# First layer's modulation weights with outputs on partitions, and a first attention that starts on half of its normed features

## The reference, cut to what matters

```
c_act = silu(c)                                     # [1024]
mod = c_act @ ada_w[0] + ada_b[0]                   # 6*1024 outputs
sh_a, sc_a, gt_a, sh_m, sc_m, gt_m = split(mod, 6)
h = rms_norm(x, attn_norm[0]) * (1 + sc_a) + sh_a   # [512, 1024]
mix = diff_attention(h, ...)                        # 8 heads: project q, k, v, scores, softmax, values
x = x + gt_a * mix
h = rms_norm(x, mlp_norm[0]) * (1 + sc_m) + sh_m
x = x + gt_m * squared_relu_mlp(h)
```

## Time and profile before

| what | value |
|---|---|
| median of 3 runs | 2463.81 us (2459.13 to 2465.54) |
| the profiled execution: its own time | 2467.75 us |
| its span in the trace | 2465.9 us |
| PE busy | 2325.3 us (94%) |
| DVE busy | 1139.2 us (46%) |
| ACT busy | 503.7 us (20%) |
| mean granted TensorE clock | 0.968 |

### The profile page before, as it was taken

One profiled execution on the slowest core, in us unless ns is written; L12 is line 12 of the kernel. 1 busy time (PEld: TensorE's weight loads), 2 busy tenths in 40 slices (PEclk: granted clock), 3 DMA queues, 4 the chain that ended last, 5 costly groups with the idle time before them and its releaser, 6 DMA issues. The chain is left out here.

```text
span 2465.9 us, 25652 instructions
## 1 busy us (share of the span) xinstructions
PE 2325.3 (94%) x9556; PEld 1482.2 (60%) x9556; DVE 1139.2 (46%) x2608; ACT 503.7 (20%) x1139; POOL 43.1 (2%) x50
## 2 busy tenths in 40 slices
PE   6999899999999999989999999999999999889886
PEld 4445456888888655554688888954556543333332
DVE  5444424666676256652455667568533211111004
ACT  2223202331002144441233100112323000000001
POOL 0000000000000000000000000000000000000000
PEclk9999899999999899989999999899998899999999
DMA  8444302534343111122444444411032679999995
GB/s 357 153 154 158 132 35 103 204 137 190 152 186 130 52 35 52 52 77 103 171 170 171 174 167 182 160 69 68 1 137 102 225 306 427 426 427 426 423 425 223
DMA packets 45455, 452.68 MB, mean 184 GB/s; under 512 B 7784, under 2 KB 7784, under 8 KB 20240
## 3 DMA queue, kind: packets, MB, share of 16 engines
q1 hardware_dynamic: 37616, 435.64, 44.3%
q0 software_dynamic: 6528, 12.17, 1.3%
q10 hardware_dynamic: 1184, 3.19, 0.3%
HBM read 444.54 MB, written 18.39 MB: 188 GB/s over the span
## 5 line engine op out<-in xcount | busy, mean ns | idle before, releaser
L2836 PE MATMUL ps<-ring,big 128*64 128x512 f32 (+1 forms) x768 | 233.4, 611 | 28.4 <-issue 16.1
L1127 PE MATMUL ps<-big,ring 128*128 128x256 f32 x768 | 187.3, 381 | 4.8 <-PEq L899 4.8
L514 PE MATMUL ps<-hT,ring 128*128 128x512 f32 x384 | 174.7, 606 | 2.1 <-ACT hT L431 2.1
L2836 PEld LDWEIGHTS ps<-ring,big 128*64 128x64 f32 (+1 forms) x768 | 85.4, 151 | 147.2 <-issue 134.1
L1127 PEld LDWEIGHTS ps<-big,ring 128*128 128x128 f32 x768 | 146.8, 191 | 25.7 <-issue 5.5
L919 PE MATMUL ps<-hT,ring 128*128 128x256 f32 x672 | 154.3, 379 | 1.5 <-ACT big L990 1.5
L2932 DVE TENSOR_TENSOR big<-big,ps 128x512 f32<-128x512 f32 x20 | 13.8, 688 | 295.6 <-ACT big L2901 281.5
L1917 PE MATMUL ps<-hT,ring 128*128 128x512 f32 x320 | 142.4, 600 | 2.7 <-DVE big L2299 1.7
L919 PEld LDWEIGHTS ps<-hT,ring 128*128 128x128 f32 x672 | 127.5, 190 | 20.3 <-issue 3.1
L869 DVE SCALAR_TENSOR_TENSOR ring<-ring,tmp 128x1024 f32<-128x1024 f32 x112 | 136.0, 1219 | 0.0
L2836 PE MATMUL ps<-big 128*64 128x512 f32 (+1 forms) x352 | 128.9, 600 | 7.1 <-ACT big L2897 3.3
(11 more groups left out here) (487 smaller groups left out, 3438.0 us busy)
## 6 DMA issues: line engine op xcount, KB each, us to landing
ring<-in_stream SPq DMA_DIRECT2D x99, 2048.0 KB, 8.7
ring<-in_gate SPq DMA_DIRECT2D x17, 2048.0 KB, 29.5
ring<-in_up SPq DMA_DIRECT2D x16, 2048.0 KB, 25.8
ring<-in_down SPq DMA_DIRECT2D x15, 2048.0 KB, 28.6
big<-in_up SPq DMA_DIRECT2D x9, 2048.0 KB, 25.4
big<-in_down SPq DMA_DIRECT2D x8, 2048.0 KB, 27.4
big<-in_gate SPq DMA_DIRECT2D x7, 2048.0 KB, 24.3
hT<-in_down SPq DMA_DIRECT2D x5, 2048.0 KB, 26.7
```

The lines of the kernel that those rows point to most:

```text
L514: last = pe.matmul(m.ps[:, 2 + j, :], w[:, k, j * P:(j + 1) * P], m.hT[:, k, :], start=(k == 0), stop=(k == KT - 1))
L1127: ins = pe.matmul(m.ps[:, bank[name], q * H:(q + 1) * H], a[:, q * P:(q + 1) * P], b, start=(first and q == 0), stop=(final and q == 1))
L2836: ins = pe.matmul(out[a:z, :], left[:, k * P + a:k * P + z], bufs[i % WBUF][:, k * width + c * 512:k * width + (c + 1) * 512], start=(k == ...
```

## The change

It does six things.

1. The modulation weights of the first layer are laid out with outputs on partitions (`output_rows`). A chunk still has 512 outputs, as four tiles of 128 outputs by 1024 inputs. DVE multiplies a tile by c_act laid along the free axis and takes the sum with the same instruction (`modulation_tile`), so there is no row sum on PE.
2. c_act along the free axis (`crow`, 128x1024) is made by 8 matmuls against the identity and one ACT copy at the start.
3. The first chunks are put in the order: each holds two scale tiles and two shift tiles. After c chunks, tiles 0 to 2c - 1 can be normed.
4. The start phase takes only two such chunks (`ADA_A0 = 2`). The other two are read in the attention phase by `first_rows(2)` and `first_rows(3)`, after DVE has scaled tiles 0 to 3. The stream is now: modulation 0, 1, head 0's weights (chunk 2), modulation 3, 4, 5, head 1's weights (chunk 6), modulation 7, head 2's (chunk 8), and so on.
5. PE projects head 0 with the feature tile as the outer loop and q, v, k inside (`project_first`).
6. x is loaded ahead of all chunks. In ACT's queue the squares and the root come ahead of the table transfers, and in DVE's queue the inverse root comes after the first chunk instead of after the last.

```diff
-ADA_A0 = 4
-DIFF = 2 * DIFF_HEADS
+ADA_A0 = 2
+DIFF = 2 * DIFF_HEADS + 2
+def modulation_tile(m, dve, n, j, row, out):
+    w = m.ring[:, n % RING, j * D:(j + 1) * D]
+    return dve.scalar_tensor_tensor(w, w, 1.0, row, ALU.mult, ALU.mult, accum_out=out)
+def first_column(c, j):
+    return 8 * (j % 2) + 2 * c + j // 2
+def first_gains(m, dve, c1, k0, k1):
+    pair = lambda a: a[:, 0:16].rearrange("p (a k) -> p a k", a=2)[:, :, k0:k1]
+    c1.link(dve.tensor_tensor(pair(m.mod0), pair(m.mod0), pair(fl(m, "ada_b0")), ALU.add))
+    return dve.scalar_tensor_tensor(m.gain[:, k0:k1], m.mod0[:, 8 + k0:8 + k1], 1.0, fl(m, "attn_norm0")[:, k0:k1],
+                                    ALU.add, ALU.mult)
...
                 sp.dma_start(m.vec[:], m.d_vec).then_inc(small, 16)
-                load_stream(m, sp, 0, 1)
                 sp.dma_start(m.con[:], m.d_con).then_inc(consts, 16)
-                load_stream(m, sp, 1, 2)
                 sp.dma_start(m.xT[:], m.d_x.rearrange("(k p) t -> p k t", p=P)).then_inc(xin, 16)
-                load_stream(m, sp, 2, RING)
+                load_stream(m, sp, 0, RING)
                 prefetch(m, sp, "ada_a")
...
+                for c in range(n):
+                    chunk, full, v = ring_chunk(m, at + c)
+                    dve.wait_ge(full, v)
+                    for j in range(4):
+                        o = first_column(c, j)
+                        modulation_tile(m, dve, at + c, j, crow, m.mod0[:, o:o + 1]).then_inc(mod_done, 1)
+                    dve.wait_ge(mod_done, 4 * (c + 1))
+                    dve.sem_inc(m.free[(at + c) % RING], 1)
+                    if c == 0:
                         dve.wait_ge(rooted, 1)
                         dve.reciprocal(m.st[:, 0:NT], m.st[:, 0:NT]).then_inc(inverse, 1)
+                first_gains(m, dve, c1, 0, 2 * n)
...
+        def weights(h):
+            return at if h == 0 else at + 2 + 2 * h
+        def modulations(h):
+            return at + 3 + 2 * h
...
                 n0 = at + RING
-                load_stream(m, sp, n0, n0 + 2)
+                load_stream(m, sp, n0, n0 + 3)
                 for h in range(2, heads):
                     sp.wait_ge(biased, 8 * h - 8)
                     load_rel(h)
-                    for n in (n0 + 2 * h - 2, n0 + 2 * h - 1):
+                    for n in (n0 + 2 * h - 1, n0 + 2 * h):
                         load_stream(m, sp, n, n + 1)
-                load_stream(m, sp, n0 + 14, n0 + 16)
+                load_stream(m, sp, n0 + 15, n0 + DIFF)
...
+                def project_first():
+                    n = weights(0)
+                    w = m.ring[:, n % RING, :].rearrange("p (k n) -> p k n", k=8)
+                    pe.wait_ge(m.full[n % RING], 16 * (n // RING + 1))
+                    for k in range(KT):
+                        pe.wait_ge(h_ok, k + 1)
+                        for j in (0, 2, 1):
+                            ins = pe.matmul(m.ps[:, 2 + j, :], w[:, k, j * P:(j + 1) * P], m.hT[:, k, :],
+                                            start=(k == 0), stop=(k == KT - 1))
...
-                    pe.wait_ge(acc_ready, h + 1)
-                    if h:
-                        pe.wait_ge(mod_done, h)
-                    sum_rows(m, pe, acc[:, h % 2, :], m.ps[:, 7, 0:4], 4).then_inc(row_sum, 1)
                     pe.wait_ge(v_tok, h + 1)
...
+                def first_rows(c):
+                    n = at + c - 1
+                    dve.wait_ge(m.full[n % RING], 16 * (n // RING + 1))
+                    for j in range(4):
+                        o = first_column(c, j)
+                        modulation_tile(m, dve, n, j, crow, m.mod0[:, o:o + 1]).then_inc(mod_done, 1)
+                    dve.wait_ge(mod_done, 4 * (c - 1))
+                    dve.sem_inc(m.free[n % RING], 1)
+                    c1.link(first_gains(m, dve, c1, 2 * c, 2 * c + 2))
+                    scale_rows(m, dve, outs, hs, (2 * c, 2 * c + 1))
...
-                scale_rows(m, dve, outs, hs)
+                scale_rows(m, dve, outs, hs, range(4))
+                first_rows(2)
+                first_rows(3)
                 c1.link(dve.tensor_scalar(m.sub[:], fl(m, "subln"), 1.0 - LAM_INIT, None, ALU.mult))
                 k_evac(0)
                 for h in range(heads):
-                    bias(h, 3)
-                    modulate(h, 0, 3)
-                    bias(h, 2)
-                    modulate(h, 3, 6)
-                    bias(h, 1)
-                    modulate(h, 6, 8)
-                    bias(h, 0)
+                    for j in range(4):
+                        bias(h, 3 - j)
+                        modulate(h, j)
```

More of the change, by code:

```diff
@@ L199, in prefetch, with condition_rows @@
     load_stream(m, sp, at + RING, at + n + RING)
[L202 to L216, removed]
+def condition_rows(m):
+    return m.big[:, 13568:13568 + D]
+def modulation_tile(m, dve, n, j, row, out):
[8 more added lines that the diff above has]
+                                    ALU.add, ALU.mult)
 def phase_start(nc, m):
@@ L283, in _ @@
                 dve.tensor_reduce(m.lam[:, 0:2], lt, AX.X, ALU.add).then_inc(lamc, 1)
-                dve.wait_ge(sig, 2)
+                dve.wait_ge(sig, 3)
                 c1.link(dve.tensor_tensor(m.lam[:, 2:3], m.lam[:, 1:2], m.lam[:, 0:1], ALU.subtract))
                 c1.link(dve.tensor_scalar(m.lam[:, 3:4], m.lam[:, 2:3], -LAM_INIT, None, ALU.add))
-                for i in range(n):
-                    chunk, full, v = ring_chunk(m, at + i)
-                    dve.wait_ge(full, v)
[L290 to L302, removed]
@@ L317, in _ @@
                 pe.wait_ge(m.go, 3)
[L318 to L325, removed]
-                    pe.wait_ge(acc_ready, i + 1)
-                    if i >= 2:
-                        pe.wait_ge(mod_done, i - 1)
-                    sum_rows(m, pe, acc[:, i % 2, :], m.ps[:, 1 + i % 2, 0:4], 4).then_inc(row_sum, 1)
+                for k in range(KT):
+                    pe.wait_ge(sqd, k + 1)
+                    for j in range(NT):
+                        last = pe.matmul(m.ps[:, 3 + j, 0:1], m.hT[:, k, j * P:(j + 1) * P], m.ones[:, 0:1],
+                                         start=(k == 0), stop=(k == KT - 1))
+                last.then_inc(summed, 1)
                 pe.wait_ge(inverse, 1)
@@ L413, in keep_busy, with scale_rows @@
         pe.matmul(m.ps[:, bank, 0:P], con(m, "ident"), con(m, "ident"), start=True, stop=True)
-def scale_rows(m, dve, outs, scaled):
+def scale_rows(m, dve, outs, scaled, tiles=range(KT)):
     for j, (_, out) in enumerate(outs):
-        for k in range(KT):
+        for k in tiles:
             dve.scalar_tensor_tensor(out[:, k, :], m.xT[:, k, :], m.gain[:, 8 * j + k:8 * j + k + 1], m.ps[:, 7, :],
@@ L580, in _ @@
                 half = KT // 2
-                for j in (0, 2, 1):
-                    project(0, j, 0, KT)
+                project_first()
                 v_rows(0)
@@ L3319, in arrays_of @@
     out = {}
-    ada0 = chunks(I["ada_w"][0])
+    w = np.asarray(I["ada_w"][0]).reshape(D, 48, P)
+    in_turn = [a + k for k in range(8) for a in (0, 8)] + list(range(16, 48))
+    ada0 = output_rows(w[:, in_turn].reshape(D, 48 * P))
     w = I["a_w_in"][0].reshape(D, 3, DIFF_HEADS, P)
```

84 lines of the change are left out of this document (41 added, 43 removed).

## The result

The changed kernel takes 2445.24 us (median of 4 runs, 2441.51 to 2446.21) against 2464.68 of the kernel before (4 runs, 2459.13 to 2468.4). The ratio is 0.992, with a 95% interval of 0.9901 to 0.9939. That is 19.4 us faster. The forecast was 2452.4 and its range ended at 2447, so the direction is right, and the gain was undersized by more than a third. The profiled execution took 2444.82 (span 2443.0); the one before took 2467.75 (span 2465.9), so the spans differ by 22.9 where the sum said 11.4. Over all sets of runs the kernel before took 2456.7 to 2469.4 us, with granted clocks from 0.973 down to 0.968, and both of its traces come from the upper end (2467.75 and 2468.66).

A forecast was written before the change was run, and what follows sets the result against it. TensorE, busy 94% of the span, was taken as the bound. The terms -10.8 + 5.8 + 2.6 - 5.7 - 3.3 = -11.4 us gave 2452.4 us from the median 2463.81, range 2447 to 2460.

The forecast's parts named there:

- What bounds the kernel, and the start: TensorE, busy 94% of the span; at the start, earlier scaling and first projection save 10.8 us.
- The new wait: Before head 1's projection: its weights wait for the slot head 0's weights occupy, costing 5.8 us, upper bound 15.7.
- The clock behind it: In head 1, after PE's idle stretch: lower TensorE clock costs 2.6 us, with 0 and 3.4 as ends.
- Chunks 6 to 8 sharing the engines: Rival, at head 1's weights: three chunks loaded evenly, chunk 6 lands 9.9 us later, time 2462; chance 0.09.
- The row sums: Between v's transposes and the values, seven full heads: removing eight PE instructions, 0.81 us a head, saves 5.7 us.
- The last head: Where PE waits on DVE: 1.8 us less DVE chain and 1.5 of row sums, together -3.3, ends 1.3 and 4.5.
- DVE's chain: In the last head, first modulation piece to reciprocal: 7.95 us instead of 9.75, so -1.8.
- The later phases shift as a whole: After the last head: same slots, loads and order, so these phases only move in time; no gain or loss.
- The rival of the clock that stays low: After the wait in head 0, PE stays at the lower level through head 1: +16 us, time 2480; chance 0.04.
- better luck in the last head: The last head reaches its best end, 4.5 us saved instead of 3.3; 1.2 allowed in the range.

The follow-up runs named there:

- the filled hole: Six filler matmuls of 512 columns put into PE's idle wait before head 1's projection, against the changed kernel; 2441.11 us, ratio 0.9897.

## Why the prediction was right in most of its steps and wrong in its size

- *What bounds the kernel, and the start.* Right. The arrivals, the 13.1 us of squares' sums, DVE's stand at the root and the phase's end came as worked out; the term was 1.1 too small, because the sums took 13.11 instead of 13.79 and the first projection 22.75 instead of 23.20.
- *The new wait.* Right in place and price: 5.7 measured for 5.8. The kernel with a free slot for head 1 shows that the shared slot alone makes it. The clock behind it was 2.0 for 2.6, and the filled hole shows that it is the idle that costs it.
- *Chunks 6 to 8 sharing the engines.* Did not happen: the first of the three was there 7.7 after the projection's end, as a single one had been.
- *The row sums.* Right; 0.89 a head for 0.81. Putting them back costs 6.25 in seven heads.
- *The last head.* The step that failed. The forecast took -3.3 from work, 1.8 less on DVE's chain and 1.5 of row sums, and left the clock of this stretch as it was. The term measured -8.6. Of that, 4.1 are clock: from the values on, both kernels do the same work, and the values took 2.91 instead of 4.62, the eight sums 1.05 instead of 1.87 and the spread 3.81 instead of 5.41. In the kernel before half clock stood for some 27 us, in the changed one for some 10. Filling the kernel before's last head gave a net 4.3 back without taking any work away. The row sums gave 1.6, as forecast (values 2.2 after the transposes instead of 3.8). DVE's chain was mis-sized: the transposes come 13.20 after the first scores instead of 16.07, 2.9 for 1.8. The forecast kept most of the 1.3 us that DVE stood between its pieces (0.22, 0.22, 0.30 and 0.56), and these went too: its reciprocal comes 6.88 after the first piece (277.84 - 270.96), where 7.95 was forecast and 9.75 stood before. In the kernel without the early start 0.93 of this gain is lost again, because DVE waits for scores that run at the low clock.
- *The later phases shift as a whole.* The second step that failed, by 3.9. Over all kernels the same instructions took 2137.4 to 2153.6. The clock can be read for this. In each trace I took the time for which PE was busy while half clock was granted, from the residual phase on: 113.0 us before, 103.6 in the changed kernel, 78.7 with the early start undone. Half of it is an estimate of what the low level cost there, since the same instructions take about twice as long at it (transposes 2.40 and 1.26). Without that half these phases take 2096.6, 2097.5 and 2098.0 us, and 2094.0 to 2099.6 over all fourteen traces. So the clock accounts for most of the 16 us between kernels and for all of the 3.9. That the later phases differ by some 3.9 in both pairs of traces (2153.1 and 2149.3, 2153.6 and 2149.7) is partly luck, for single phases of the changed kernel moved between its two executions: the second MLP took 414.9 and 418.0, the mixing phase 228.0 and 224.5.
- *The rival of the clock that stays low* was put behind the hole, and did not happen there: after the hole the level was back within six microseconds. Something like it was already in the kernel before, in the last head, and the change took most of it away.

The range ended 1.8 above the result. It allowed 1.2 us for better luck in the last head, and nothing for the clock of later phases.

Open: what sets where the level falls and returns. The same kernel gives the same stretch again (34.0 and 34.1; 25.4 and 25.5). Kernels with the same last head give 25.4 to 29.6 when something earlier differs, and the moment at which they reach it does not order them. Less work, row sums taken out, and earlier arrival all changed it, and no run separates what the removed one-column matmuls did from what the changed place did. With the last head counted up to its values (2.9 + 1.6 = 4.4 from unrounded figures), the measured terms give 11.9 + 6.3 + 4.4 - 5.7 - 2.0 = 14.9 us; the other 8.0 of the 22.9 in the traces are clock in stretches that the change did not set out to touch.

The Trainium skill (TensorE: Matmul & The Clock Gate, What's actually happening) holds that the number of slow matmuls at a kernel's start differs from run to run, and that one should not fit to a certain count. The traces show the like behind the hole of head 0: with 5.6 to 6.0 us of idle before them, the same eight instructions took 5.41 to 6.25 us. In the last head two executions each of two kernels agree to 0.12 us; two are few.

## What to carry to other kernels

When a consumer is moved forward in a stream that goes through a ring, check for each later chunk whose reader frees its slot: here two heads in a row came to share one, which took 7.7 us of a head start of 11.9 us, and one exchange of two chunks gave it back. When a stretch of waits on small matmuls gets shorter, price it at both clock levels and give the range the difference; here it was 4.1 us, about as much as the work. And with changes of some 10 us in such a kernel compare milestones, not totals: phases that no edit touched moved by up to 16 us.

## What the runs showed that I had not expected

TensorE kept its lower level for some 27 us although it was busy for 3.75 to 4.70 of every 5 us in the second half of that time (windows above). In the first trace transposes, row sums and values ran from 294.87 to 303.25 without a gap, 8.4 us, and the level did not rise. Seven matmuls that nobody reads made the kernel before 12 us faster by the median. And the same 32 spread instructions took 3.81 to 6.46 us in kernels that differ only in what came before them.
